# Blocks of x, gate and up in one transfer each; a last layer norm by halves; reciprocal roots by GpSimd's power

## The reference

```python
x = layer_norm(ALPHA * x + 0.5 * swiglu(x, gate1, up1, down1), g1, b1)
h = x @ w_in                     # q, k, v for 8 stick-breaking and 8 chunked heads
x = layer_norm(ALPHA * x + mixed_heads(h) @ w_out, g2, b2)
x = layer_norm(ALPHA * x + 0.5 * swiglu(x, gate2, up2, down2), g3, b3)

def swiglu(x, w_gate, w_up, w_down):
    return (silu(x @ w_gate) * (x @ w_up)) @ w_down      # inner width 2816

def layer_norm(x, g, b):
    mu = mean(x)
    var = mean((x - mu) ** 2)
    return (x - mu) * rsqrt(var + 1e-5) * g + b
```

## Time and profile before

| | us |
|---|---|
| median of three runs | 976.34 |
| the profiled execution | 977.56 |
| its span | 975.8 |
| PE busy | 963.2 (99%) |
| DVE busy | 809.4 (83%) |
| ACT busy | 562.9 (58%) |
| POOL busy | 21.2 (2%) |
| chain that ended last | PE 84%, DVE 10%, ACT 3% |

### The profile page before, as it was taken

How to read it: one execution, slowest core, us unless ns; L and a number is a source line. 1 busy time by engine, 2 the same in 40 slices (tenths; PEclk the granted TensorE clock), 3 DMA queues, 4 the chain that set the end, 5 groups by cost and what they waited for, 6 DMA issues and landing times.

```text
span 975.8 us, 16987 instructions
## 1 busy us (share of the span) xinstructions
PE 963.2 (99%) x6570; PEld 884.1 (91%) x6570; DVE 809.4 (83%) x892; ACT 562.9 (58%) x623; POOL 21.2 (2%) x53
## 2 busy tenths in 40 slices
PE   9999999999999999999999999999999999999996
PEld 9899999899778999999899999998987789999996
DVE  5998887855898998887889988878558889988885
ACT  5755554558884655554566555545688656555543
POOL 1000000001000000000000000000010000000000
PEclk9999999999999999999999999999999999999999
DMA  8766654662343656454626574544642536655444
GB/s 302 256 222 253 218 172 171 215 240 106 131 163 139 216 192 237 173 211 174 219 98 211 209 301 172 216 173 173 216 147 99 180 136 216 241 173 212 171 170 153
DMA packets 34651, 187.27 MB, mean 192 GB/s; under 512 B 3888, under 2 KB 3888, under 8 KB 19504
## 3 DMA queue, kind: packets, MB, share of 16 engines
q1 hardware_dynamic: 33120, 177.22, 51.0%
q0 software_dynamic: 1488, 9.45, 2.5%
HBM read 185.61 MB, written 1.05 MB: 191 GB/s over the span
## 4 chain that ended last, share of the span: by engine, by line
PE 84%; DVE 10%; ACT 3%; issue 2%; DMA 1%; POOL 0%; SPq 0%; DVEq 0%; POOLq 0%; ACTq 0%
PE bank L1225 25%; PE bank L1226 25%; PE bank L1227 25%; PE bank L1366 7%; DVE w_lo L809 3%; ACT w_hi L458 2%; PE bank L1288 1%; DMA raw<-stream 1%; DVE soft_t L1103 1%; DMA kT<-first 1%; DVE mx L1106 1%; DVE stick_t L1085 1%; POOL stick_t L417 0%; DVE soft_t L1119 0%; DVE soft_t L1123 0%
## 5 line engine op out<-in xcount | busy, mean ns | idle before, releaser
L1225 PE MATMUL bank<-xT_hi,w_hi 128*128 128x256 f32 x1456 | 412.2, 283 | 0.0
L1227 PE MATMUL bank<-xT_hi,w_lo 128*128 128x256 f32 x1456 | 412.0, 283 | 0.0
L1226 PE MATMUL bank<-xT_lo,w_hi 128*128 128x256 f32 x1456 | 412.0, 283 | 0.0
L458 ACT ACTIVATE w_hi<-raw 128x2048 fp32r<-128x2048 f32 x120 | 229.1, 1912 | 132.9 <-PE bank L1227 127.4
L1225 PEld LDWEIGHTS bank<-xT_hi,w_hi 128*128 128x128 f32 x1456 | 279.1, 192 | 3.7 <-issue 0.7
L1226 PEld LDWEIGHTS bank<-xT_lo,w_hi 128*128 128x128 f32 x1456 | 279.2, 192 | 3.0
L1227 PEld LDWEIGHTS bank<-xT_hi,w_lo 128*128 128x128 f32 x1456 | 279.1, 192 | 0.0
L803 DVE TENSOR_TENSOR w_lo<-raw,w_hi 128x2048 fp32r<-128x2048 f32 x87 | 199.2, 2290 | 45.1 <-ACT w_hi L458 44.8
L1225 PE MATMUL bank<-w_hi,h_hi 128*128 128x512 f32 x284 | 111.8, 394 | 1.5 <-DVE soft_t L972 1.1
L1226 PE MATMUL bank<-w_lo,h_hi 128*128 128x512 f32 x284 | 111.4, 392 | 0.0
L1227 PE MATMUL bank<-w_hi,h_lo 128*128 128x512 f32 x284 | 110.5, 389 | 0.0
(11 more groups left out here) (166 smaller groups left out, 1233.8 us busy)
## 6 DMA issues: line engine op xcount, KB each, us to landing
raw<-stream SPq DMA_DIRECT2D x110, 1024.0 KB, 4.9
raw<-stream SPq DMA_DIRECT2D x112, 512.0 KB, 4.6
lnp<-ln_gb POOLq DMA_DIRECT2D x6, 1024.0 KB, 5.6
band<-rel_band POOLq DMA_DIRECT2D x2, 1024.0 KB, 9.1
qT<-first SPq DMA_DIRECT2D x2, 512.0 KB, 4.0
kT<-first SPq DMA_DIRECT2D x2, 512.0 KB, 6.6
xn<-x POOLq DMA_DIRECT2D x1, 1024.0 KB, 5.3
out<-xn SPq DMA_DIRECT2D x4, 256.0 KB, 2.0
```

Of the source, the lines that this page charges most:

```text
L458: nc.scalar.activation(w_hi[:, at(slot if into is None else into)], raw[:, slot, :], ACT.Copy).then_inc(hi_ready, 1)
L1225: nc.tensor.matmul(o, w[0], x[0], start=start, stop=False, skip_group_check=again)
L1226: nc.tensor.matmul(o, w[0], x[1], start=False, stop=False, skip_group_check=again)
L1227: return nc.tensor.matmul(o, w[1], x[0], start=False, stop=stop, skip_group_check=again)
```

## The change

It has three parts.

1. **Opening.** The input `first` now holds x, gate 0 and up 0 in five chunks: two of one 128-row block, three of two blocks, each 128 x (768 or 1536) floats with the part of x, of gate and of up side by side. They land in qT (twice), kT, v and band. Up 0 has no load of its own, so unit 3 and unit 4 are the first to use raw slots 0 and 1. PE takes gate's and up's products chunk by chunk into two banks. ACT and DVE split three pieces for each chunk. DVE's order after it is new: gated product and sums before unit 3, which is split in halves; the low part of h before the weight sums; and in step 0 of the loop gated product before unit 5. The fp32r copy of the tables (`neg_r`) moves from the opening behind ACT's split of unit 5, and PE's fill has eight products.
2. **Reciprocal root.** In all six norms ACT's Ln and Exp and DVE's three operations go. POOL computes var + eps (`root`) and raises it to -0.5 (`power`). POOL does both blocks of a norm in turn; in each layer the loads of gains and band come behind the first norm's roots.
3. **Last norm** (`last_norm`). PE finishes half 0 of the second block before half 1. DVE adds that half before it normalises the first block, and forms minus twice the sum over D, the half's own mean. ACT squares that half around its own mean, and later the other half around the whole mean. POOL joins them: with d the difference of the two means, the first half's sum grows by 512 d^2 (`joined_root`).

```diff
-            for q in range(4):
-                sp.dma_start(quarter[q], first_in[:, q, :]).then_inc(QUARTER_READY[q], 16)
-            for c, ready in zip(HALVES, (u0_half_ready, raw_ready[1])):
-                sp.dma_start(raw[:, 1, c], stream[1][:, c]).then_inc(ready, 16)
+            for q, (k0, k1) in enumerate(CHUNKS):      # (0,1) (1,2) (2,4) (4,6) (6,8)
+                sp.dma_start(chunk[q], first_in[:, 768 * k0:768 * k1]).then_inc(chunk_ready[q], 16)
...
@@ GpSimd
+            def power(tb, n):
+                wait_alone(lnv_done, n + 1)
+                nc.gpsimd.tensor_tensor(lt[:, tb, 1:2], lt[:, tb, 0:1], eps[:, 2:3], ALU.pow).then_inc(rstd_done, 1)
+            def root(l, p):
+                for tb in range(2):
+                    n = phase(l, p) * 2 + tb
+                    if n == 6 * DEPTH - 1:
+                        joined_root(n)
+                    else:
+                        wait_alone(var_done, n + 1)
+                        nc.gpsimd.tensor_scalar(lt[:, tb, 0:1], sums[:, tb, 3:4], 1.0 / D, LN_EPS,
+                                                ALU.mult, ALU.add).then_inc(lnv_done, 1)
+                    power(tb, n)
+            def joined_root(n):
+                wait_alone(half_var, 1)
+                wait_alone(ln_step, n * LN_STEPS + LN_MEAN)
+                nc.gpsimd.tensor_scalar(tail[:, 2:3], tail[:, 0:1], sums[:, 1, 2:3], None,
+                                        ALU.subtract).then_inc(tail_step, 1)
+                wait_alone(tail_step, 1)
+                nc.gpsimd.tensor_scalar(tail[:, 3:4], tail[:, 2:3], tail[:, 2:3], D / 2.0,
+                                        ALU.mult, ALU.mult).then_inc(tail_step, 1)
+                wait_alone(tail_step, 2)
+                nc.gpsimd.tensor_scalar(tail[:, 4:5], tail[:, 3:4], tail[:, 1:2], D * LN_EPS,
+                                        ALU.add, ALU.add).then_inc(tail_step, 1)
+                wait_alone(tail_step, 3)
+                wait_alone(var_done, n + 1)
+                nc.gpsimd.tensor_scalar(lt[:, 1, 0:1], sums[:, 1, 3:4], tail[:, 4:5], 1.0 / D,
+                                        ALU.add, ALU.mult).then_inc(lnv_done, 1)
@@ GpSimd, per layer
                 load_lnp(l, 0)
+                root(l, 0)
                 pool.dma_start(mixg[:, :], mix_g[l]).then_inc(att_par, 16)
                 pool.dma_start(band[:, :, :], rel_band[l]).then_inc(att_par, 16)
...
+                root(l, 1)
                 load_lnp(l, 2)
+                root(l, 2)
@@ ScalarE, last norm, second block
+                    act.wait_ge(half_mean, 1)
+                    nc.scalar.activation(ez[:, 0, :], xn[:, 1, 0:512], ACT.Square, bias=tail[:, 0:1],
+                                         accum_out=tail[:, 1:2]).then_inc(half_var, 1)
+                    act.wait_ge(ln_step, n * LN_STEPS + LN_MEAN)
+                    nc.scalar.activation(ez[:, 1, :], xn[:, 1, 512:1024], ACT.Square, bias=sums[:, 1, 2:3],
+                                         accum_out=sums[:, 1, 3:4]).then_inc(var_done, 1)
@@ ScalarE, opening
+            for q in range(len(CHUNKS)):
+                act.wait_ge(chunk_ready[q], 16)
+                nc.scalar.activation(xT_hi[:, CHUNKS[q][0]:CHUNKS[q][1], :], x_chunk(q),
+                                     ACT.Copy).then_inc(x_chunk_hi, 1)
+                for s in range(2):
+                    nc.scalar.activation(w_hi[:, at(s, w_chunk(q))], chunk_part(q, 1 + s),
+                                         ACT.Copy).then_inc(hi_ready if q == len(CHUNKS) - 1 else first_hi, 1)
@@ VectorE, opening of the first feed-forward
-                    split_lo(l, base + 3, 0)
                     gated(0, 1, bank[7], first=True)
                     h_sums(0)
+                    for half in range(2):
+                        dve.wait_ge(*((hi_ready, 4) if half else (first_hi, FIRST_HALVES + 2)))
+                        split_half_lo(half)
+                    low_h(0)
                     weight_sums(l, f, 0, FILLED[base + 1] + 1)
                     split_pure_lo(l, f, 0)
-                    low_h(0)
                     split_differences_lo(l, f, 0)
...
+                    if j == 0 and r < 0:
+                        gated(j + 1, 3 * j + 3, bank[6])
+                        split_lo(l, base + 3 * j + 5, 2)
+                        weight_sums(l, f, j + 1, FILLED[base + 1] + 2 + j)
@@ VectorE, last norm
+                add(0, 0)
+                add(0, 1)
+                mean(0)
+                centre(0)
+                add(1, 0)
+                dve.wait_ge(ln_step, (n0 + 1) * LN_STEPS + 1)
+                nc.vector.tensor_scalar(tail[:, 0:1], sums[:, 1, 0:1], -2.0 / D, None, ALU.mult).then_inc(half_mean, 1)
+                normed(0)
+                add(1, 1)
+                mean(1)
+                centre(1)
+                normed(1)
@@ TensorE, opening
+                for q, (k0, k1) in enumerate(CHUNKS):
+                    pe.wait_ge(x_chunk_hi, q + 1)
+                    final = q == len(CHUNKS) - 1
+                    for s, into in ((0, bank[0]), (1, bank[7])):
+                        pe.wait_ge(*((hi_ready, s + 1) if final else (first_hi, 2 * q + s + 1)))
+                        last = all_three(s, into, range(k0, k1), 0 if s else q + 1,
+                                         (lo_ready, split(0, s)) if final else (first_lo, 2 * q + s + 1))
@@ TensorE, last step of the last feed-forward
+                if count + 1 == 3 * DEPTH:
+                    for half in range(2):
+                        pair(1, (h_hi, h_lo), 1, half)
+                        pair(2, hl, 1, half, True).then_inc(y_done, 1)
@@ TensorE, start
-            fill(9)
-            pe.wait_ge(consts, 10)
+            fill(8)
+            pe.wait_ge(consts, 11)
```

More of the change, by code:

```diff
@@ L211, in trunk @@
         x_loaded = sem("x_loaded")
-        quarter_ready = [sem(f"quarter_ready{q}") for q in (0, 2)]
-        u0_half_ready = sem("u0_half_ready")
+        chunk_ready = [sem(f"chunk_ready{q}") for q in range(5)]
+        x_chunk_hi = sem("x_chunk_hi")
+        x_chunk_lo = sem("x_chunk_lo")
         g1_half_ready = sem("g1_half_ready")
@@ L312, in trunk, with chunk_part, x_chunk, w_chunk @@
         HALVES = [slice(0, UW // 2), slice(UW // 2, UW)]
[L313 to L318, removed]
+        CHUNKS = ((0, 1), (1, 2), (2, 4), (4, 6), (6, 8))
+        chunk = [flat(qT)[:, 0:768], flat(qT)[:, 768:1536], flat(kT)[:, 0:1536], flat(v)[:, 0:1536],
+                 flat(band)[:, 0:1536]]
+        def chunk_part(q, i):
+            n = CHUNKS[q][1] - CHUNKS[q][0]
+            return chunk[q][:, 256 * n * i:256 * n * (i + 1)]
+        def x_chunk(q):
+            return chunk_part(q, 0).rearrange("p (c t) -> p c t", t=T)
+        def w_chunk(q):
+            return slice(256 * CHUNKS[q][0], 256 * CHUNKS[q][1])
+        FIRST_HALVES = 2 * (len(CHUNKS) - 1)
         def loaded(l, slot, filled):
-            return l * (16 * PER_LAYER[slot]) + 16 * (filled + 1)
+            return l * (16 * PER_LAYER[slot]) + 16 * (filled + (1 if slot == 2 else 0))
         block = ctx.enter_context(nc.Block())
@@ L504, in rstd @@
                                      accum_out=sums[:, tb, 3:4]).then_inc(var_done, 1)
-                act.wait_ge(var_done, n + 1)
-                nc.scalar.activation(lt[:, tb, 0:1], sums[:, tb, 3:4], ACT.Ln, scale=1.0 / D,
-                                     bias=eps[:, 0:1]).then_inc(lnv_done, 1)
-                act.wait_ge(lnv_done, n + 1)
-                nc.scalar.activation(lt[:, tb, 1:2], lt[:, tb, 0:1], ACT.Exp, scale=-0.5).then_inc(rstd_done, 1)
             def after_ln(l, p):
@@ L550, in ffn @@
                 if r < 0:
[L551 to L555 removed]
+                    for half, c in enumerate(HALVES):
+                        act.wait_ge((g1_half_ready, raw_ready[2])[half], 16)
+                        nc.scalar.activation(w_hi[:, at(2, c)], raw[:, 2, c],
+                                             ACT.Copy).then_inc((first_hi, hi_ready)[half], 1)
                     silu(0, 0)
[L557 removed]
+                    for half, c in enumerate(HALVES):
+                        act.wait_ge((half_ready, raw_ready[0])[half], 16)
+                        nc.scalar.activation(w_hi[:, at(0, c)], raw[:, 0, c],
+                                             ACT.Copy).then_inc((first_hi, hi_ready)[half], 1)
                     high_h(0)
@@ L576, in ffn @@
                 split_hi(l, base + 5, 2, first[2] + 1)
+                if r < 0:
+                    act.wait_ge(consts, 11)
+                    nc.scalar.activation(neg_r[:, :, :], table[:, 1:4, :], ACT.Copy).then_inc(neg_ready, 1)
                 def step(j):
@@ L1691 @@
     stream = weight_stream(ins)
-    first = np.stack([x.reshape(T, 4, 2, P).transpose(3, 1, 2, 0).reshape(P, 4, 512),
-                      stream[0].reshape(P, 4, 512)], 2).reshape(P, 4, 1024)
+    parts = [x.reshape(T, KC, P).transpose(2, 1, 0)] + [stream[i].reshape(P, KC, 256) for i in range(2)]
```

(2 more changed lines are left out.)

160 lines of the change are left out of this document (86 added, 74 removed).

## The result

The change made the kernel slightly slower. Median 977.77 us (976.65 to 980.08, 15 runs) against 976.34 (975.64 to 977.62, 15 runs) for the kernel before: ratio 1.0015, 95% interval 1.0008 to 1.0022, or 0.8 to 2.1 us. The forecast was 974.2, with a range up to 976.6. The profiled execution took 978.38 (span 976.7), 0.8 over that of before; both lie above their medians, by 0.6 and 1.2.

A forecast was written before the change was run, and what follows sets the result against it. PE was taken to bound the kernel from 45.05 to 962.90 us and DVE from 23.75 to 45.05. Gains of 0.05 + 1.84 + 0 + 0.2 = 2.1 us from 976.34 gave 974.2, range 972.8 to 976.6.

The forecast's parts named there:

- The stages and the middle: From 45.05 to 962.90 us PE is busy 916.20 of 917.85; only the opening and last 12.9 us can gain.
- The power: POOL's power in each norm's reciprocal root: taken as 0.4 us, allowed 0.1 to 1.5.
- the band's load: Held back by POOL until the first norm is over, sharing queues with projection weights: taken as 0, at most 1.0 us.
- The first call: First power call loading its code: 5.7 us lost by the skill page's estimate, 979.9; chance 0.03.
- Chunks: Opening, x, gate and up in one transfer per chunk: 0.05 us gained; bounds 0.7 to 0.9 gained, 0.6 lost.
- DVE's lead: Opening: gated product and sums before unit 3's split put DVE's chain 2.25 us ahead, less 0.07 for one more instruction.
- rival 2: Opening: unit 3 lands after 21, so DVE's lead is missing; 0.7 us gained, 975.4 with the tail; chance 0.22.
- 1.84: Us gained in the opening if both PE stalls, 1.30 and 0.54, go; 0.7 without DVE's lead.
- The last norm: Last norm by halves, joined on POOL: 0.2 us gained, bounds -1.4 to +0.9.
- ports free: Last norm, POOL not held up by DVE's centring: 0.6 us gained.
- one hold-up: Last norm, POOL's second small operation waits for DVE's centring until about 970.75: 0.3 us lost at a power of 0.4.
- The handover from one operation of POOL to its next: In the reciprocal root's stretch, between POOL's tensor scalar and power: 0.06 us.

The follow-up runs named there:

- e10_quarters: Kernel before with unit 3's load not waiting for unit 0's split, plus DVE's new order; four quarters, old norms and roots: 975.86 us, ratio 0.9989.
- e2_early_loads: Changed kernel with the first layer's loads of units 3 and 4 issued right behind gate 1, without waiting for the first splits: 976.75 us, ratio 1.0000.
- e1_old_tail: Changed kernel with the last norm as before (whole squares, old orders), POOL's root kept in all six norms: 977.01 us, ratio 1.0003.
- e8_after_again: The changed kernel itself, measured and profiled a second time: 978.13 us, ratio 1.0013.
- e4_pool_first: Changed kernel with DVE's centring of the last block held until POOL's three offset operations are over: 977.91 us, ratio 1.0016.
- e11_no_offset: Changed kernel without POOL's three small operations for the offset between the half means, so its last variance lacks that term: 976.75 us, ratio 0.9997.
- e12_e5_again: Changed kernel with early loads of units 3 and 4 and the old last norm, POOL's roots kept; second round, another chip: 975.86 us, ratio 0.9992.
- e6_act_roots: Changed kernel with early loads of units 3 and 4, the old last norm, and roots back on ACT and DVE: 975.68 us, ratio 0.9994.
- e7_pool_roots: Kernel before with its reciprocal roots by GpSimd and nothing else new: 976.12 us, ratio 0.9993.
- e5_early_and_old_tail: Changed kernel with early loads of units 3 and 4 and the old last norm, POOL's roots kept; first round: 975.47 us, ratio 0.9983.
- e3_dve_order: Kernel before with only DVE's new order in the opening and step 0, unit 3 split in halves: 976.33 us, ratio 0.9992.
- e9_unit3_only: Kernel before with one edit, unit 3's load no longer waiting for unit 0's split: 975.88 us, ratio 0.9990.

## Why the prediction was wrong

*The stages and the middle: right.* Only the two ends moved; PE's list of waits in the middle begins with the same two entries of 0.7 and 0.4 us in both traces. The power was put at 0.4 and took 0.56; the band's load, issued behind the first norm, cost nothing visible. The first call is like the others (0.57). The Trainium skill, "GPSIMD Engine Reference", section 2.1, gives about 6 us more for the first call of a freshly loaded kernel; this power routine shows no such call.

*Chunks: inside the bounds, and no more can be said.* First product at 5.51 instead of 5.1 to 5.4; PE then waits for chunk three, and resumes at 9.89 instead of 9.28. A landing at 8.6 and 0.6 lost was the bound on that side. In the nine traces with five chunks the third piece is read at 7.26 to 8.97, after 8.4 in four of them; in the five with four quarters at 7.36 to 7.99. So the chunks may land later on average. Whether they do stays open: the times of e10_quarters and of the versions with chunks don't tell them apart.

*DVE's lead: the step that failed.* The sum had unit 3 issued at 14.1 (its own terms, 12.12 + 1.1 + 0.8, give 14.0), its halves landing at 17.8 and 19.1, DVE 2.25 ahead, `h_lo` done at 39.9. Issue was at 14.55 and the halves were read at 19.20 and 21.64. I had taken the issue-to-landing time of the kernel's very first transfer, 3.65 us, although the trace held the row for this very load: from issue at 11.43 to the reading at 18.61, 7.2 us. 14.55 + 7.2 would be 21.7. The measured second half is 21.64. What I gave 0.22 as rival 2 is what happened, and even it was too kind: with 1.03 and 0.47 us of new idle time on DVE, the first stall didn't shrink but moved into the second, and 1.84 became 0.

The agreement of 7.2 and 7.1 us is partly luck. Rival 2 explained the long time by a load that stands behind others. It did stand behind others before, but in the changed kernel the transfer engines were all but idle from 13 to 16 us, and it took as long. After its issue come those of units 4 and 5 (from 16.50), whose bytes move beside its second half; whether that makes it long was not tested.

There is a second term that the prediction put at nothing: unit 7, which DVE's weight sums of the next step read. The new order has the low part of h (1.0 us) before the sums and the split that free unit 7's slot, and no longer behind them. So DVE asks for unit 7 5.25 us after its issue (26.78 to 32.03 in the trace of e2_early_loads), and before it was 6.27 (28.70 to 34.97). Among the eleven traces with the new order DVE waits for unit 7 in eight, 0.47 to 1.03 us, and in those it is read 5.8 to 6.4 after its issue; in the three with the old order it never waits. This decides how much of the stall the late load of unit 3 explains. Where the third chunk came at 8.6 (the first trace and e1_old_tail), unit 3 was issued at 14.5, DVE waited 1.03 and 1.05 for it, and PE's stall was 1.46 and 1.97. Where it came at 7.4 to 7.6 (e8_after_again, e4_pool_first, e11_no_offset), unit 3 was issued at 13.3 to 13.6, DVE didn't wait for it, and PE still waited 0.6 to 0.9, behind DVE's wait for unit 7 (0.72 to 0.83) alone. No run moves the load of unit 7 by itself.

That an earlier load of unit 3 is worth 1.4 us is shown by the times; that it is also most of the gain that the reordering was credited with was not seen at all. SP's wait for unit 0's split was itself a cost of the kernel before.

*The last norm: the sign.* Between +0.6 (ports free) and -0.3 (one hold-up) I took +0.2; it was -1.0. Three sizes were off. The handover from one operation of POOL to its next was put at 0.06 and is 0.18 to 0.21, up to 0.30: five operations in a chain pay it four times, 0.89 in sum. The power is 0.57. And the centring holds up two operations, not one. Each POOL operation that reads SBUF beside the centring ends just after the DVE operation that it fell on: L443 at 970.24 (the first centring ends about 970.07), L446 at 970.87 (the second ends 970.74). The Trainium skill, "SBUF — State Buffer", section "Who interferes with whom", says that a VectorE operation with two SBUF inputs and a GpSimd operation that reads SBUF contend for a port pair that is locked exclusively; the traces agree for GpSimd's side, by 0.75 against 0.31 and 0.78 against 0.57. VectorE's centring isn't lengthened (1.42 in all of them).

*The sum.* Forecast: 2.1 us gained. Opening 1.9 less than thought and tail 1.2 less make 1.0 lost; 1.4 was measured (0.8 to 2.1). The remaining 0.4 lies within that. Undoing the tail gives back about 1.1 and the load about 1.4 (ratios 1.0003 and 1.0000 against a mean of 1.0014 for the changed kernel's two), and both together 2.6. Taken the other way, the load is worth 1.5 with the old tail and the tail 1.2 with the early loads. Each of these is uncertain by about 1, but the tail's microsecond stands in every trace: from where the centring can start to the scaling it is 3.44 to 3.48 with the full join, 2.46 or 2.47 with the whole block. With both mended the kernel is 1.2 below before, not 2.1: the stalls are gone in some executions and 0.7 in others, and a late third chunk costs time by itself (e12_e5_again and e6_act_roots have no stall near 41; read at 8.97 the span is 975.0, read at 7.62 it is 973.1, though they differ in the roots too). Another possible part of the loss, in no sum, is a slow start of PE's products, told at the end. Why single executions differ by up to 1.7 us in when the third chunk lands stays open.

## What to carry to other kernels

When an edit moves the event that releases a load, price the load by its own issue-to-landing time in the old trace and not by that of the first transfer (7.2 us against 3.65 here; in the changed kernel 7.1), and look first whether it needs to wait for that event at all: here a load released for a free slot was worth as much as the whole reordering. A wait that disappears from the profile has not been won until the next thing that the same engine hands over is earlier too. When work moves ahead in an engine's order, ask of each later load how long after its issue it is now wanted: here 5.25 us instead of 6.27, and it mostly took longer. And count short operations on GpSimd by spacing, about 0.4 to 0.5 us each with their handover (a power 0.75), and more beside a VectorE operation with two SBUF operands.

## What the runs showed of the hardware

- The small multiplication of `mixg` (128 x 8), 0.23 us before, takes 2.25 in the changed kernel. Nothing about it changed but its moment: it starts 0.14 after a DVE split of two SBUF operands (199.70 to 201.99) and ends at 202.09, just behind it. DVE and POOL in the changed kernel:

```profile
199.70 4.58 DVE L865 TENSOR_TENSOR w_lo<-raw,w_hi 128x2048 fp32r<-128x2048 f32 x2 [1.11 <-ACT w_hi L508]
...
202.04 0.52 POOL L482 MEMSET band<- 64x512 f32 x1
```

  The MEMSET behind it, which only writes, runs beside the second of the two splits in its usual 0.52. In the second trace of the changed kernel the multiplication takes 2.38. With GpSimd's roots on the kernel before, the same multiplication comes 0.02 before the split and takes 0.24.
- The third piece of the opening is read by ACT at 7.26 to 8.97 us over nine executions with five chunks (the same program: 7.39 and 8.60, or 8.44 and 8.97), though it is issued at 1.73 in all of them. With four quarters it is 7.36 to 7.99 over five.
- In both traces of the changed kernel the first products of the opening come 0.21 us apart, up to 6.9 and 7.4, and 0.12 after that. The granted clock in the row of that stretch is 1.00 all the same. All three variants with the late load show it too, and so do e12_e5_again (up to 6.7) and e7_pool_roots, which has nine fills and the old opening (up to 7.6); e5_early_and_old_tail has a trace of it. The kernel before, e2_early_loads, e3_dve_order, e6_act_roots, e9_unit3_only and e10_quarters don't. So neither the fills nor the loads alone decide it. In the first trace it hides behind chunk three, since PE waits for that anyway. In e8_after_again, e4_pool_first and e11_no_offset PE goes over into chunk three without a wait, so there it costs time. In e11_no_offset it lasts to 10.5, and the gated product starts at 19.72 instead of 18.27 (e4_pool_first, chunk three at nearly the same time). Its cause, and its part in the changed kernel's longer times, were not looked for.
